# Column sums of squares in a two-block transformer kernel: one fp32 product replaced by two fp32r products of a split operand

## The reference, cut to what matters

```python
def rmsnorm(x, g):
    xf = x.astype(jnp.float32)
    y = xf * lax.rsqrt(jnp.mean(xf * xf, axis=-1, keepdims=True) + EPS) * g.astype(jnp.float32)
...
x = x + mix @ w_out[l]
h = rms_norm(x, norm_ffn[l])
...
df_heads = differential_attention(dq, dk, dvv, lam)
df_out = (rmsnorm(df_heads, subln_norm[l]) * (1.0 - lambda_init)).reshape(B, S, DF_WIDTH)
```

## Time and profile before

| | |
|---|---|
| median of 3 runs | 1955.8 us (1955.64 to 1956.62) |
| the profiled execution | 1955.69 us |
| its span | 1953.9 us |
| mean granted TensorE clock | 0.999 |
| TensorE busy | 1923.8 us, 98% |
| VectorE, ScalarE, POOL busy | 916.7, 834.5, 881.6 us (47%, 43%, 45%) |
| DMA | 168.77 MB, mean 86 GB/s |

### The profile page before, as it was taken

One profiled execution on the slowest core, in us unless ns is written; L12 is line 12 of the kernel. 1 busy time (PEld: TensorE's weight loads), 2 busy tenths in 40 slices (PEclk: granted clock), 3 DMA queues, 4 the chain that ended last, 5 costly groups with the idle time before them and its releaser, 6 DMA issues. The chain is left out here.

```text
span 1953.9 us, 25592 instructions
## 1 busy us (share of the span) xinstructions
PE 1923.8 (98%) x9150; PEld 1510.5 (77%) x9150; DVE 916.7 (47%) x1420; ACT 834.5 (43%) x1269; POOL 881.6 (45%) x1188
## 2 busy tenths in 40 slices
PE   9999999999999999999999999999999999999998
PEld 7866766788888887777688888887777688888887
DVE  5487877432241346777541313133777643222132
ACT  4466555543242345555532223134555542222233
POOL 4322221456456465343355455454443355454543
PEclk9999999999999999999999999999999999999999
DMA  8211111233234233222134233333222223243322
GB/s 234 65 44 44 34 44 33 87 106 110 84 89 119 76 96 99 75 66 75 48 107 116 78 108 97 87 97 95 78 66 76 65 85 110 86 119 86 109 86 76
DMA packets 318100, 168.77 MB, mean 86 GB/s; under 512 B 15028, under 2 KB 313367, under 8 KB 317847
## 3 DMA queue, kind: packets, MB, share of 16 engines
q1 hardware_dynamic: 314432, 162.38, 28.9%
q10 hardware_dynamic: 3542, 4.76, 1.0%
HBM read 160.29 MB, written 2.10 MB: 83 GB/s over the span
## 5 line engine op out<-in xcount | busy, mean ns | idle before, releaser
L737 POOL TENSOR_TENSOR wlo<-raw,whi 128x256 fp32r<-128x256 f32 x1164 | 865.2, 775 | 1042.2 <-ACT whi L778 1042.2
L1621 PE MATMUL accs<-Xh,whi 128*128 128x512 f32 x1448 | 581.3, 401 | 0.1
L1623 PE MATMUL accs<-Xh,wlo 128*128 128x512 f32 x1448 | 565.1, 390 | 0.0
L1622 PE MATMUL accs<-Xl,whi 128*128 128x512 f32 x1448 | 563.9, 389 | 0.0
L778 ACT ACTIVATE whi<-raw 128x1024 fp32r<-128x1024 f32 x291 | 307.7, 1061 | 267.6 <-PE accs L1623 218.5
L1621 PEld LDWEIGHTS accs<-Xh,whi 128*128 128x128 f32 x1448 | 272.1, 188 | 58.6 <-issue 3.7
L1623 PEld LDWEIGHTS accs<-Xh,wlo 128*128 128x128 f32 x1448 | 271.8, 188 | 58.4
L1622 PEld LDWEIGHTS accs<-Xl,whi 128*128 128x128 f32 x1448 | 272.4, 188 | 56.1 <-issue 3.6
L1621 PE MATMUL accs<-Uh,whi 128*128 128x512 f32 x744 | 289.7, 389 | 0.8 <-DVE xT L1210 0.8
L1622 PE MATMUL accs<-Ul,whi 128*128 128x512 f32 x744 | 289.4, 389 | 0.0
L1623 PE MATMUL accs<-Uh,wlo 128*128 128x512 f32 x744 | 289.4, 389 | 0.0
(11 more groups left out here) (303 smaller groups left out, 1913.8 us busy)
## 6 DMA issues: line engine op xcount, KB each, us to landing
raw<-in_w_ff_dram SPq DMA_DIRECT2D x128, 512.0 KB
raw<-in_w_in_dram SPq DMA_DIRECT2D x71, 512.0 KB
raw<-in_w_gate_up_dram SPq DMA_DIRECT2D x44, 512.0 KB
raw<-in_w_down_dram SPq DMA_DIRECT2D x16, 512.0 KB
raw<-in_w_o_dram SPq DMA_DIRECT2D x16, 512.0 KB
px<-W ACTq DMA_DIRECT2D x64, 64.0 KB, 2.0
raw<-in_w_down_dram SPq DMA_DIRECT2D x8, 384.0 KB
W<-in_x_dram SPq DMA_DIRECT2D x4, 512.0 KB, 6.1
```

The costliest lines, as they stand in the source:

```text
L737: pool.tensor_tensor(lo[:, ks], raw[:, unit_no % RAW, ks], hi[:, ks].bitcast(F32), ALU.subtract).then_inc(sems["wlo"], 1)
L1621: mmul(y, whi[:, slot, k], xh[:, k], start=(i == 0), stop=False)
L1622: mmul(y, whi[:, slot, k], xl[:, k], start=False, stop=False)
L1623: last = mmul(y, wlo[:, slot, k], xh[:, k], start=False, stop=(i == len(ks) - 1))
```

## The change

The column sum is now made of two fp32r products with a matrix of ones, of the high and the low part of the operand, and the division by 1024 or 128 has moved into the scale of the Ln. For the five norms a new item `ssplit` behind the last `prep` splits `ssq`: ScalarE copies it, rounded, to `Uh[:, 0]`, VectorE subtracts into `Ul[:, 0]`. For the eight head groups ScalarE squares O twice, once rounded into `Uh[:, 4 + j]` and once into `sq`, and POOL subtracts into `Ul[:, 4 + j]`. The tile `ones_r` is filled once by VectorE. `norm0`, the norms of q and k and that of the recurrence's heads keep their products.

```diff
     if last:
         out.append(("prep", c, ("cur", c)))
-        return out
+        return out + ([("ssplit",)] if last else [])
...
@@ gpsimd
+                elif item[0] == "dv":
+                    c = 4 + item[1]
+                    pool.wait_ge(sems["O_act"], at("O_act", 1))
+                    pool.tensor_tensor(Ul[:, c], sq[:, :], Uh[:, c].bitcast(F32), ALU.subtract).then_inc(sems["s_lo"], 1)
...
@@ scalar
+                elif kind == "ssplit":
+                    act.wait_ge(sems["sq"], at("sq"))
+                    act.wait_ge(sems["xl"], at("xl"))
+                    A(Uh[:, 0], ssq[:, :], ACT.Copy).then_inc(sems["s_hi"], 1)
+                    act.wait_ge(sems["s_hi"], at("s_hi", 1))
...
-                    A(rstd[:, :], M[:, :], ACT.Ln, bias=eps).then_inc(sems["M_act"], 1)
+                    if kind == "norm":
+                        A(rstd[:, :], M[:, :], ACT.Ln, bias=eps, scale=1.0 / D).then_inc(sems["M_act"], 1)
+                    else:
+                        A(rstd[:, :], M[:, :], ACT.Ln, bias=eps).then_inc(sems["M_act"], 1)
...
                     act.wait_ge(sems["ul"], at("oy_read"))
+                    A(Uh[:, 4 + item[1]], O[:, :], ACT.Square).then_inc(sems["s_hi"], 1)
+                    act.wait_ge(sems["s_hi"], at("s_hi", 1))
                     A(sq[:, :], O[:, :], ACT.Square).then_inc(sems["O_act"], 1)
...
-                    A(rs, M[:, :], ACT.Ln, bias=eps).then_inc(sems["M_act"], 1)
+                    A(rs, M[:, :], ACT.Ln, bias=eps, scale=1.0 / P).then_inc(sems["M_act"], 1)
...
@@ vector
+                elif kind == "rounds":
+                    dve.wait_ge(sems["ld_const2"], 16)
+                    CP(ones_r[:, :], ones).then_inc(sems["ones_r"], 1)
+                    dve.wait_ge(sems["ones_r"], 1)
+                elif kind == "ssplit":
+                    dve.wait_ge(sems["s_hi"], at("s_hi", 1))
+                    TTn(Ul[:, 0], ssq[:, :], Uh[:, 0].bitcast(F32), ALU.subtract).then_inc(sems["s_lo"], 1)
+                    dve.wait_ge(sems["s_lo"], at("s_lo", 1))
...
@@ tensor
+            def column_sums(c):
+
+                pe.wait_ge(sems["ones_r"], 1)
+                pe.wait_ge(sems["s_lo"], at("s_lo"))
+                mmul(M[:, :], ones_r[:, :], Uh[:, c], start=True, stop=False)
+                return mmul(M[:, :], ones_r[:, :], Ul[:, c], start=False, stop=True)
...
-                    mmul(M[:, :], o1024, ssq[:, :], start=True, stop=True).then_inc(sems["M_fill"], 1)
+                    column_sums(0).then_inc(sems["M_fill"], 1)
...
-                    pe.wait_ge(sems["O_act"], at("o_sq"))
                     pe.wait_ge(sems["M_act"], at("M_act"))
                     pe.wait_ge(sems["M_dve"], at("M_dve"))
-                    mmul(M[:, :], o128, sq[:, :], start=True, stop=True).then_inc(sems["M_fill"], 1)
+                    column_sums(4 + item[1]).then_inc(sems["M_fill"], 1)
```

More of the change, by code:

```diff
@@ L96 @@
     "params1": dict(prm=1), "params2": dict(M_fill=1, M_act=1), "first": dict(),
-    "xin": dict(S_fill=1, S_act=1, xh=1, xl=1), "xsq": dict(), "xsum": dict(x_sum=1), "warm": dict(), "split": dict(), "loads": dict(), "cmpc": dict(cmp_c=1),
+    "xin": dict(S_fill=1, S_act=1, xh=1, xl=1), "xsq": dict(), "xsum": dict(x_sum=1), "warm": dict(), "split": dict(), "loads": dict(), "rounds": dict(ones_r=1), "cmpc": dict(cmp_c=1),
     "prep": dict(sq=1, xh=1, xl=1),
-    "norm": dict(M_fill=1, M_act=1, rstd=1), "norm0": dict(M_fill=1, M_act=1, rstd=1),
+    "ssplit": dict(s_hi=1, s_lo=1), "norm": dict(M_fill=1, M_act=1, rstd=1), "norm0": dict(M_fill=1, M_act=1, rstd=1),
     "mmA": dict(), "mmB": dict(unit=1), "mmK": dict(),
@@ L137 @@
     "d1": dict(T_fill=1, T_dve=1, T_act=1), "d2": dict(p_ok=1), "d3": dict(T_fill=1, T_act=1),
-    "dv": dict(O_fill=1, O_act=1), "on1": dict(M_fill=1, M_act=1, o_r=1, o_y=1), "on2": dict(uh=1, ul=1),
+    "dv": dict(O_fill=1, O_act=1, s_hi=1, s_lo=1), "on1": dict(M_fill=1, M_act=1, o_r=1, o_y=1), "on2": dict(uh=1, ul=1),
     "nat": dict(S_fill=1, S_act=1), "gload": dict(), "wn": dict(), "grp": dict(unit=1, acc=1, sq=1), "fin": dict(fin_r=1, y0=1, y1=1),
@@ L189, in marks_of @@
     if kind == "dv":
-        return dict(at_read="O_fill", o_sq="O_act")
+        return dict(at_read="O_fill")
     if kind == "on1":
@@ L332, in outputs @@
         s += [("prep", n, (kind, at + n)) for n in ready]
-    return s
+    return s + [("ssplit",)]
 X, SQ, HI = (lambda c: ("x", c)), (lambda b, h: ("xsq", b, h)), (lambda n: ("split", n))
@@ L362, in block1 @@
     s += [("mmA", u(C_VW)), ("nq2", 5, R_KN + 2), ("mmB", u(C_VW)), ("cmp2k",), ("vt",)]
-    s += [("mmA", u(C_G)), ("cmp1", 1), ("mmB", u(C_G)), ("vt2", "vw"), ("ga",)]
+    s += [("mmA", u(C_G)), ("cmp1", 1), ("mmB", u(C_G)), ("vt2", "vw"), ("ga",), ("rounds",)]
     cols = {"hi": C_HI, "hg": C_HG, "hf": C_HF, "hq": C_HQ}
@@ L510 @@
         "ga_ok", "ga_x", "g_ok2", "c_x", "c_e", "c_ok", "n_ok", "n_uh", "p_ok", "pv", "f_ok", "f_ln", "ha_b", "ha_d", "ha_e", "ha_k", "hl_d", "hl_e", "hl_f",
-        "o_r", "o_y", "uh", "ul", "u_new", "sb_l", "sb_w", "rp", "y0", "y1", "fin_r", "ld_gain", "yg", "x_sq", "x_sum"]
+        "o_r", "o_y", "uh", "ul", "u_new", "sb_l", "sb_w", "rp", "y0", "y1", "fin_r", "ld_gain", "yg", "x_sq", "x_sum", "s_hi", "s_lo", "ones_r"]
 LANDED = 96
@@ L537, in build @@
         rows, vec = sb("rows", [P, P]), sb("vec", [P, NROWS])
+        ones_r = sb("ones_r", [P, P], F32R)
         masks = sb("masks", [P, 4, P], BF16)
```

## The result

The kernel after takes 1974.54 us (median of 4 runs, 1973.91 to 1976.05), the kernel before, run beside it, 1956.21 us: the ratio is 1.0093, 95% interval 1.0075 to 1.011. So it is slower by 18.3 us where 12.6 was forecast, and 1.0 us above the forecast's range.

What follows compares the result with a forecast made beforehand. TensorE, busy 98% of the span, was taken as the bound. Norms -2.1, middle sites +1.4, dv 2 +7.0, dv 3 +3.0 and clock +3.3 gave +12.6 us on 1955.7: 1968.3 us, range 1962.8 to 1973.5.

Steps and rivals of the forecast that it cites:

- what decides: POOL's queue at the eight dv/on1 sites: POOL stops until O is squared, so the next wlo comes later.
- A (covered): Rival: POOL's wait is covered and only the cheaper sums are left, -5.5 us, 1950.2 us; chance 0.04.
- D (swallowed later): Rival: TensorE's later waits swallow much of the shift and the clock holds, +3.9 us, 1959.6 us; chance 0.04.
- B: Rival: the same waits, but the clock holds, +9.3 us, 1965.0 us; chance 0.30.
- the wait at dv 2: Two sites with output projection pieces behind them, which need all four wlo parts: +3.5 us each, +7.0 for two.
- the clock's term: Granted clock falls to half at both dv 2 waits of about 5 us: 1.65 us twice, +3.3 us.
- dv 3 without a fall: Two sites at the end of a layer, where the sum waits for POOL: +1.5 us each, +3.0 for two.
- the middle sites: Four dv sites in the middle of a layer: next unit's wlo slightly late, +0.35 us each, +1.4 for four.
- the norms and the products: fp32r pairs 0.23 us apart save 0.42 us a sum; five norm sites don't wait, -2.1 us.
- Rival C: Dearer: POOL at its slow rate or clock down for longer; 1977 at all sites, 1972.6 at half that excess; chance 0.15.

Runs made afterwards that it cites:

- The wait alone: Kernel before with only POOL's wait for ScalarE's square added in its dv step, no arithmetic changed: 1967.0 us, ratio 1.0056.
- last site fp32: Kernel after with the last head group's sum of each layer (dv 3) in plain fp32 again, one square, no POOL step: 1969.1 us, ratio 1.0069.
- filled kernel: Kernel after with 20 products that nobody reads issued by TensorE in the wait at dv 2: 1968.2 us, ratio 1.0066.
- parts-ahead kernel: Kernel after, but POOL makes the next unit's wlo before it waits for the square of dv 0, 1 and 2: 1957.76 us, ratio 1.0006.
- norms-only kernel: Kernel after with dv and on1 as before, only the five norms as split sums: 1955.57 us, ratio 0.9998.

## Why the prediction was right in kind and short in size

**Right: what decides.** POOL's step stands ahead of the next `wlo` in an in-order queue. The wait alone costs 11.2 us, and the parts made ahead of it give 16.8 back. Rivals A (covered) and D (swallowed later) are out. So is B: the clock didn't hold.

**Right: the wait at dv 2.** Forecast +3.5 a site; filled, the site costs 3.8 and 3.9. POOL runs at its quiet pace: 1.27 us and 0.70 a part where 1.5 and 0.8 were taken, so the piece starts at 935.56 (935.65 forecast, though the square itself is 0.2 later).

**Failed: the size of the clock's term.** The step was "products done in as long a stretch would lose half of it. I take that, 1.65 us, twice". The 3.3 us stretch was only where before's record ends, not how long a fall lasts. Behind the 4.7 us waits the clock stays at half for 10.2 us, all four times that a profile shows (after, and the last site fp32), and the price is 3.0 us a site by the filled kernel. That is 2.7 us too little in the sum. The Trainium skill (TensorE: Matmul & The Clock Gate, "HAM oscillation") gives 1.67 us of throttled time a burst; here it is 10.2 us, six times as much, so for waits in work like this the measurement decides and that figure is not a bound.

**Failed: dv 3 without a fall.** The step costed these sites at +1.5 and the clock term named only "both sites" of 5 us. The wait is 2.1 us (+1.6, right), and in after it brought a fall both times, 3.4 us long and worth 1.7. That is 3.4 us missing. The forecast read 2.7 us, the delay at the end of the trace, as a span that a wait must exceed. It was one fall, not a limit: shorter waits brought falls as well.

**Failed, small: the middle sites**, forecast at +0.35 each. The table has 0.1 us for two of them in the first layer and 0.4 for the two in the second, with POOL at its quiet pace (1.30 us for the subtraction of the first). That is 0.9 us too much.

**Right: the norms and the products.** Nine pairs 0.23 us apart (the other four sit at the lower clock or behind a wait), no wait at a norm, -0.40 us each at the first two norms in the trace where -0.42 was forecast. That the five make the kernel faster by 2.1 us isn't shown by times.

The corrected sum is -2.1 + 0.5 + 2 x (3.85 + 3.0) + 2 x (1.6 + 1.7) = +18.7 us, measured 18.3; after's own runs spread over 2.1. The waits at dv 2 and dv 3 were taken 0.9 us too low together and the middle sites 0.9 too high, so these misses cancel by luck, and the whole shortfall is the clock's. Rival C named it ("the clock is down for longer") but priced only POOL's slow pace, which did not occur; that its 1972.6 and 1977 lie around the measured time is luck too.

## What to carry to other kernels

Before an engine that feeds others is given a new step with a late operand, list what stands behind that step in its queue and make it ahead of the wait: here one waiting line on an engine that is busy 45% of the time cost 11 us, falls of the clock included, and moving one tile's low half, four short instructions, over each such step gave back 16.8 of 18.3. Price an idle gap of TensorE as the gap plus the clock that it may cost, and don't take the length of a fall from a record that ends in it. A cheaper form of an operation is worth it only where its operand is early: with the parts ahead, going back to the dear form at the one place without slack took another 4.3 us off, and the rest then beats the kernel before by 2.2.

## What was not expected of the hardware

How long the clock stays at half varied with more than the wait before it. It was 10.2 us behind each of four 4.7 us waits, 6.8 and 10.2 us behind two waits of 3.25 us, and 3.4 us behind three of the 2.1 us waits.

The same wait brings a fall in one profile and none in another. In the profiled runs, of the 2.1 us waits at dv 3 after's were followed by a fall 2 times in 2, the kernel's filled at dv 2 once in 2, the parts-ahead kernel's never in 2. In the norms-only kernel the clock fell for 3.4 us behind waits of 0.53 and 0.91 us at d1, although before's profile holds 1.00 behind 1.10 and 0.91 us. What tells these apart no run here shows. Behind none of the six waits filled with products did it fall.

The kernel before isn't free of this, it seems. Of the 40 times that it ran beside the experiments, 13 have a mean granted clock of 0.998 and take 1957.2 us on average; the other 27 have 0.999 or 1.000 and take 1955.6. That is about the price of one fall, though none of the 13 was profiled.
